# The input projection by Strassen's seven products, in two passes over paired column blocks

## What is computed

```python
h = rmsnorm(x, norm_mix_g)                      # (1024, 2048)
proj = h @ w_in                                 # (1024, 6160)
na_q, na_k, na_v, ml_q, ml_k, ml_v, ml_o, gates = split(proj)
na_out = rmsnorm(neighbourhood_attention(na_q, na_k, na_v))
ml_out = mlstm_mixer(conv(ml_q, ml_k), ml_v, sigmoid(ml_o), gates)
x = x + concat(na_out, ml_out) @ w_out          # (1024, 2048)
x = rmsnorm(x + expert_choice_ffn(rmsnorm(x)))  # 16 experts of 128 tokens
```

## Time and profile before

| | us |
|---|---|
| median of three runs | 2886.12 |
| span of the profiled execution, first to last instruction | 2884.0 |
| PE busy | 2791.8, 97% of the span |
| DVE busy | 1616.2, 56% |
| ACT busy | 1328.0, 46% |
| bytes moved | 665.67 MB, mean 231 GB/s |

### The profile page before, as it was taken

How to read it: one execution, slowest core, us unless ns; L and a number is a source line. 1 busy time by engine, 2 the same in 40 slices (tenths; PEclk the granted TensorE clock), 3 DMA queues, 4 the chain that set the end, 5 groups by cost and what they waited for, 6 DMA issues and landing times.

```text
span 2884.0 us, 33947 instructions
## 1 busy us (share of the span) xinstructions
PE 2791.8 (97%) x12906; PEld 2301.7 (80%) x12906; DVE 1616.2 (56%) x1801; ACT 1328.0 (46%) x1465; POOL 392.4 (14%) x613
## 2 busy tenths in 40 slices
PE   9999999999999999989999967999999999999997
PEld 7888888788888888767888856888888888888884
DVE  4111111321332326676345658888888888888886
ACT  6111112211111106654333334777777777777775
POOL 1200000020110024572010101000000000000002
PEclk9999999999999999999999988999999999999998
DMA  8322112121423237533444457999999999999997
GB/s 322 90 80 80 59 65 78 54 96 56 150 96 104 92 107 229 193 123 129 153 164 142 166 166 312 381 403 403 393 396 404 403 405 402 405 401 405 401 390 336
DMA packets 193313, 665.67 MB, mean 231 GB/s; under 512 B 23305, under 2 KB 48408, under 8 KB 170016
## 3 DMA queue, kind: packets, MB, share of 16 engines
q1 hardware_dynamic: 168336, 564.52, 51.6%
q0 software_dynamic: 24848, 99.46, 10.1%
HBM read 591.06 MB, written 75.76 MB: 231 GB/s over the span
## 4 chain that ended last, share of the span: by engine, by line
PE 91%; DVE 2%; POOL 2%; DMA 2%; issue 2%; ACT 1%; POOLq 0%; SPq 0%; DVEq 0%; ACTq 0%
PE ps L2275 24%; PE ps L1950 18%; PE ps L1929 6%; PE ps L1928 6%; PE ps L1930 6%; PE ps L2298 4%; PE ps L2297 4%; PE ps L2296 4%; PE ps L2202 4%; PE ps L2204 4%; PE ps L2203 4%; PE ps L2020 1%; PE ps L2000 1%; PE ps L2251 1%; DMA nak<-scr_feats 1%
## 5 line engine op out<-in xcount | busy, mean ns | idle before, releaser
L1843 DVE TENSOR_TENSOR elo<-eraw,ehi 128x2048 fp32r<-128x2048 f32 x384 | 874.2, 2291 | 131.2 <-ACT ehi L1263 124.4
L1263 ACT ACTIVATE ehi<-eraw 128x2048 fp32r<-128x2048 f32 x384 | 732.9, 1919 | 248.6 <-PE ps L2275 162.3
L1356 DVE TENSOR_TENSOR wlo<-raw,whi 128x1024 fp32r<-128x1024 f32 x95 | 116.4, 1225 | 684.5 <-ACT whi L999 684.4
L999 ACT ACTIVATE whi<-raw 128x1024 fp32r<-128x1024 f32 x95 | 100.6, 1059 | 718.8 <-PE ps L1950 381.7
L2275 PE MATMUL ps<-ehi,xh 128*128 128x512 f32 x960 | 373.6, 389 | 0.0
L2275 PE MATMUL ps<-elo,xh 128*128 128x512 f32 x960 | 373.5, 389 | 0.0
L1928 PE MATMUL ps<-whi,a_hi 128*128 128x512 f32 x768 | 299.0, 389 | 3.0 <-DVE a_lo L1377 3.0
L1930 PE MATMUL ps<-whi,a_lo 128*128 128x512 f32 x768 | 298.8, 389 | 0.0
L1929 PE MATMUL ps<-wlo,a_hi 128*128 128x512 f32 x768 | 298.8, 389 | 0.0
L2275 PE MATMUL ps<-ehi,xl 128*128 128x512 f32 x960 | 256.6, 389 | 0.0
L1950 PE MATMUL ps<-a_hi,whi 128*128 128x512 f32 x768 | 236.9, 389 | 2.2 <-DVE t L1399 1.6
(11 more groups left out here) (298 smaller groups left out, 3892.7 us busy)
## 6 DMA issues: line engine op xcount, KB each, us to landing
eraw<-in_w_gate SPq DMA_DIRECT2D x256, 512.0 KB, 6.1
eraw<-in_w_up SPq DMA_DIRECT2D x256, 512.0 KB, 8.2
eraw<-in_w_down SPq DMA_DIRECT2D x128, 1024.0 KB, 10.5
raw<-in_w_stream SPq DMA_DIRECT2D x95, 512.0 KB, 3.5
oraw<-in_w_stream SPq DMA_DIRECT2D x128, 256.0 KB, 2.6
scr_rows<-stage POOLq DMA_DIRECT2D x48, 256.0 KB, 2.3
scr_feats<-stage POOLq DMA_DIRECT2D x44, 256.0 KB, 2.3
t<-in_xT SPq DMA_DIRECT2D x16, 512.0 KB, 5.5
```

The source lines that it names most:

```text
L1263: act.activation(ehi[:, p % ERING, :], flat2(eraw[:, 2 * (p % EDEEP):2 * (p % EDEEP) + 2, :]), ACT.Copy)\
L1843: dve.tensor_tensor(elo[:, p % ERING, :], flat2(eraw[:, 2 * (p % EDEEP):2 * (p % EDEEP) + 2, :]), ehi[:, p % ERING, :].bitcast(F32), ALU.s ...
```

## The change

The twelve blocks are taken as six pairs q (1024 columns each). With the tokens, the contraction and a pair's columns each in two halves, the product of a pair is a 2x2 by 2x2 block product, and it is made by Strassen's seven products (m1 to m7) in place of eight. A product is 8 slices x 4 banks x 3 = 96 matmuls in four chunks; products use the banks 0 to 3 and 4 to 7 in turn, and a bank must be drained two products later (`bank_free`).

- Pass one makes, for q = 0 to 5, m4 = A22(B21-B11), m3 = A11(B12-B22), m2 = (A21+A22)B11, m5 = (A11+A12)B22. From these C21 = m2+m4 and C12 = m3+m5 are finished and stored, and m2-m3 and m5-m4 are parked in DRAM (`part`).
- Pass two makes, for q in the order 3, 0, 2, 4, 5, 1, m1 = (A11+A22)(B11+B22), m6 = (A21-A11)(B11+B12), m7 = (A12-A22)(B21+B22), loads the parked tiles and finishes C22 and C11.
- The combined inputs of pass two (24 pairs of slices, `ops`) are made by DVE and ACT during pass one (q = 1 to 4, six each), stored to DRAM, and loaded by POOL's queue at the chunks 88 to 103. Those of pass one are made from the loaded slices at the start, where the slices come as 128x512 tiles and the ones that are summed come two by two.
- The combined weights are made when they are needed: of 168 chunks, 120 are a sum or difference of two raw chunks (`PAIRED`), which DVE forms (`combine`, 128x1024). So 288 chunks are loaded in place of 96. `raw` stays a ring of four loads; `whi` and `wlo` are rings of three.
- The gate products stand before q = 5 of pass one; the gate arithmetic is at DVE's chunks 102 to 110 of pass two (before: in block 6), the convolution at the chunks 117, 123, ..., 159. A chunk is 24 matmuls now (before: 48).
- The loops of the projection are written out. Semaphores of early stages are used again by late ones (`LATER`, `BEFORE`). Attention's queries and keys come from q = 4 and 5; the queries are put in their order by the access pattern of PE's moving operand (`unit_order`, runs of 16 elements) and of the drain.

```diff
 BW = 512
 BLK = 12
-ROWBLK = 6
+NQ = BLK // 2
+ROWQ = 3
 OBLK = 4
+KH = KD // 2
 CPB = KD // 2
-RING = 4
-GWC = KD * 16 + 32
+RING, SPL = 4, 3
+GWC = 4 * P + 28
 QR, QC, WR, WC = 8, 16, 12, 32
...
+ORDER2 = (3, 0, 2, 4, 5, 1)
+QUERYQ = 4
+PRODS = [(a, q) for q in range(NQ) for a in ("m4", "m3", "m2", "m5")] + [(a, q) for q in ORDER2 for a in ("m1", "m6", "m7")]
+NP1, NPR = 4 * NQ, 7 * NQ
+NCH = 4 * NPR
+HALVES = {"m4": ((0, 4), (0, 0)), "m3": ((1, 0), (1, 4)), "m2": ((0, 0),), "m5": ((1, 4),),
+          "m1": ((0, 0), (1, 4)), "m6": ((0, 0), (1, 0)), "m7": ((0, 4), (1, 4))}
+LOADS = [(2 * PRODS[c // 4][1] + side, m + c % 4, c) for c in range(NCH) for side, m in HALVES[PRODS[c // 4][0]]]
...
+SLOT = {"m4": 3, "m3": 0, "m2": 2, "m5": 1, "m1": 3, "m6": 0, "m7": 2}
+OPSLOT = (3, 0, 2)
+OPAT = (0, 3, 5, 8, 11, 13)
+CONVAT = [117 + 6 * n for n in range(8)]
+DRAINED = (2, 3, 0, 1)
...
+        def chunk_used(eng, c):
+            p, m = c // 4, c % 4
+            if m == 3:
+                eng.wait_ge(S["bank_ready"], 4 * p + 4)
...
+        def drained(c):
+            p, i = (c - 2) // 4 - 1, (c - 2) % 4
+            if p < 0:
+                return None, None, None, None
+            a, q = PRODS[p]
...
+            def fetch(n):
+                b, m, c = LOADS[n]
+                if n >= RING:
+                    sp.wait_ge(S["w_lo"], LOADS[n - RING][2] + 1)
+                sp.dma_start(raw[:, n % RING, :], t["w_stream"][CPB * b + m, :, :]).then_inc(rawsem[n % RING], 16)
...
+            def fetch_slice(s):
+                hi, lo = slice_f32(s)
...
+                if s >= 2 * KH:
+                    sp.dma_start(hi, t["xT"][k * P:(k + 1) * P, half_ * BW:(half_ + 1) * BW]).then_inc(xtsem[s % 8], 16)
+                if s // KH != 1:
+                    k += KH
+                sp.dma_start(lo, t["xT"][k * P:(k + 1) * P, half_ * BW:(half_ + 1) * BW]).then_inc(xtsem[s % 8], 16)
...
+            def fetch_op(o):
+                if o >= 2:
+                    sp.wait_ge(opstsem[o % 2], 32 * (o // 2))
+                for a, (k, half_) in zip(op_tiles(o), op_slice(o)):
+                    sp.dma_start(a, t["xT"][k * P:(k + 1) * P, half_ * BW:(half_ + 1) * BW]).then_inc(opldsem[o % 2], 16)
...
+            def load_p11(r, i):
+                j = DRAINED[i]
+                sp.wait_ge(stsem[j], 16 * NQ + 16 * r)
+                sp.wait_ge(heldsem[j], 16 * (ORDER2[r] + 1))
+                sp.dma_start(stage[:, j, :], t["part"][0, ORDER2[r], j, :, :]).then_inc(xtsem[4 + j], 16)
...
+            def store_sum(q, j, i):
+                pool.wait_ge(S["sig_out" if q == ROWQ - 1 else "c21_out"], i + 1 if q == ROWQ - 1 else 4 * q + i + 1)
+                pool.dma_start(place_of(q, 0, 1, j), ring[0]).then_inc(S["c21_st"], 16)
+                pool.wait_ge(S["p22_out"], 4 * q + i + 1)
+                pool.dma_start(t["part"][1, q, j, :, :], ring[1]).then_inc(S["p22_st"], 16)
...
+            def load_operand(o, i):
+                part, k = i % 2, 2 * (i // 2)
+                if i == 0:
+                    pool.wait_ge(S["bank_ready"], 4 * (4 * (NQ - 1) + o + 1))
+                    for m in opstsem:
+                        pool.wait_ge(m, 32 * 4 * (o + 1))
+                pool.dma_start(slots[OPSLOT[o]][part][:, k:k + 2, :], t["ops"][o, part, k:k + 2, :, :].rearrange("k p c -> p k c"))\
+                    .then_inc(opinsem[o], 16)
...
+            def high(c):
+                n = FIRST[c]
+                if PAIRED[c]:
+                    act.wait_ge(S["w_sum"], SUMS[c])
+                else:
+                    act.wait_ge(rawsem[n % RING], 16 * (n // RING + 1))
+                if c >= SPL:
+                    chunk_used(act, c - SPL)
+                act.activation(whi[:, c % SPL, :], raw[:, n % RING, :], ACT.Copy).then_inc(S["w_hi"], 1)
...
+            def opened(tile, done, count):
+                act.wait_ge(S[done], count)
+                act.activation(tile, tile, ACT.Sigmoid).then_inc(S["sig_out"], 1)
...
+                if c == 102:
+                    act.wait_ge(S["gate_arg"], 1)
+                    act.activation(t2[0:64, 0:1024], t2[0:64, 0:1024], ACT.Exp, scale=-1.0).then_inc(S["act_step"], 1)
+                    step.settle()
+                    act.activation(t2[0:64, 0:1024], t2[0:64, 0:1024], ACT.Ln, bias=1.0).then_inc(S["gate_act"], 1)
...
+            def combine(c):
+                if not PAIRED[c]:
+                    return
+                for n in (FIRST[c], FIRST[c] + 1):
+                    dve.wait_ge(rawsem[n % RING], 16 * (n // RING + 1))
+                a, b = raw[:, FIRST[c] % RING, :], raw[:, (FIRST[c] + 1) % RING, :]
+                dve.tensor_tensor(a, a, b, sign(c)).then_inc(S["w_sum"], 1)
...
+            def sum_feats(q, j, i):
+                dve.wait_ge(S["bank_ready"], 4 * p1_at("m2", q) + j + 1)
+                dve.wait_ge(S["p22_st"], 16 * (4 * q + i))
+                dve.tensor_tensor(by_unit(ring[1], q), by_unit(bank_of(p1_at("m2", q), j), q), bc_for(q, 1), ALU.mult)\
+                    .then_inc(S["dve_step"], 1)
+                step.settle()
+                dve.wait_ge(S["s4_out"], 4 * q + 4)
+                dve.wait_ge(S["c21_st"], 16 * (4 * q + i))
+                dve.wait_ge(S["p11_out"], 4 * q)
+                dve.tensor_tensor(ring[0], ring[1], held[:, j, :], ALU.add).then_inc(S["c21_out"], 1)
+                dve.wait_ge(S["s3_out"], 4 * q + 4)
+                dve.tensor_tensor(ring[1], ring[1], stage[:, j, :], ALU.subtract).then_inc(S["p22_out"], 1)
...
+            def op_sum(o):
+                dve.wait_ge(S["rstd_bc_in"], 16)
+                dve.wait_ge(opldsem[o % 2], 32 * (o // 2 + 1))
+                for a, (k, half_) in zip(op_tiles(o), op_slice(o)):
+                    dve.scalar_tensor_tensor(out=a, in0=a, scalar=gmix[:, k:k + 1], in1=bc_half(half_), op0=ALU.mult, op1=ALU.mult)\
+                        .then_inc(S["dve_step"], 1)
+                step.settle()
+                step.settle()
+                a, b = op_tiles(o)
+                dve.tensor_tensor(a, a, b, ALU.add if o < KH else ALU.subtract).then_inc(S["op_sum"], 1)
...
+            def both_less(r, j, i):
+                p = p2_at("m1", r)
+                dve.wait_ge(S["bank_ready"], 4 * p + j + 1)
+                dve.wait_ge(xtsem[j], XT0 + 16 * (r + 1))
+                dve.tensor_tensor(held[:, j, :], bank_of(p, j), held[:, j, :], ALU.subtract).then_inc(S["q22_out"], 1)
+                dve.wait_ge(xtsem[4 + j], XT0 + 16 * (r + 1))
+                dve.tensor_tensor(stage[:, j, :], bank_of(p, j), stage[:, j, :], ALU.subtract).then_inc(S["q11_out"], 1)
...
+            def forget_sums():
+                dve.wait_ge(S["gate_act"], 1)
+                dve.scalar_tensor_tensor(out=T1, in0=T1, scalar=0.0, in1=T2, op0=ALU.min, op1=ALU.subtract).then_inc(S["dve_step"], 1)
...
+                dve.wait_ge(S["mask_done"], 1)
+                for r, way in ways:
+                    dve.tensor_tensor_scan(out=t1[r, ::way], data0=t3[r, :], data1=t1[r, ::way], initial=0.0,
+                                           op0=ALU.mult, op1=ALU.add).then_inc(S["dve_step"], 1)
+                    step.settle()
+            def running_maxima():
+                dve.tensor_tensor(T0, T0, T1, ALU.subtract).then_inc(S["dve_step"], 1)
...
+                dve.tensor_scalar(T3, T3, -1.0, -NEG, ALU.add, ALU.mult).then_inc(S["dve_step"], 1)
...
+            for c in range(1, NCH):
+                low(c)
+                if c + 1 < NCH:
+                    combine(c + 1)
...
+                drain(c)
+                if op_at(c, 0) is not None:
+                    op_sum(op_at(c, 0))
+                if op_at(c, 1) is not None:
...
+                if c == 102:
+                    gate_rows()
+                if c == 103:
+                    forget_sums()
+                if c == 104:
+                    running_maxima()
+                if c == 106:
+                    chunk_ends()
+                if c == 107:
+                    stabilizers()
+                if c == 108:
+                    dve.wait_ge(S["gate_act"], 3)
...
+            def bank_free(p, j):
+                i = DRAINED.index(j)
+                if p == 4 * (NQ - 1) and j < 2:
+                    pe.wait_ge(S["gates_copied"], 1)
+                if p < 2:
+                    return
+                a, q = PRODS[p - 2]
+                if p - 2 >= NP1:
+                    q = (p - 2 - NP1) // 3
+                pe.wait_ge(S[{"m4": "s4_out", "m3": "s3_out", "m2": "p22_out", "m5": "p11_out", "m1": "q11_out", "m6": "c22_out", "m7": "c11_out"}[a]],
+                           4 * q + i + 1)
...
+            def product(p):
+                a, q = PRODS[p]
+                slot = SLOT[a]
+                if p >= NP1:
+                    pe.wait_ge(opinsem[("m1", "m6", "m7").index(a)], 16 * 8)
...
+                    hi, lo = whi[:, c % SPL, at:at + BW], wlo[:, c % SPL, at:at + BW]
```

(16 more changed lines are left out.)

1166 lines of the change are left out of this document (657 added, 509 removed).

## The result

| | before | after | forecast |
|---|---|---|---|
| median, us | 2886.11 | 2905.88 (2903.43 to 2906.96) | 2794 (2766 to 2838) |
| span of the profiled execution | 2884.0 | 2901.7 | 2791.6 |
| first matmul of the projection | 8.65 | 10.24 | 7.9 |
| TensorE's end of the projection | 1079.7 | 1097.0 | 986.6 |
| time of TensorE beyond its matmuls | 3.7 | 150.1 | 42 |

After against before is 1.0064, 95% interval 1.0052 to 1.0076: slower by 0.6%, clear of the noise, where I had forecast 3.2% faster. (The median before is now that of four executions.) The matmuls are the 4032 + 96 forecast, and behind the projection nothing moved (2901.7 - 1097.0 = 1804.7, before 1804.3). But for a first matmul 2.3 us later than forecast, all of the miss lies in the 150.1 us, which are 1097.0 - 10.24 - 914.5 - 22.2. Products are numbered from 0, chunks from 0, four to a product.

What follows compares the result with a forecast made beforehand. It took the projection to be bound by its number of matmuls: 576 fewer save 130.6 us, some 42 return as stalls, so the projection ends at 986.6 against 1079.7, giving 2794 us (range 2766 to 2838).

Steps and rivals of the forecast that it cites:

- Weights in the steady state: Paired chunks' loads through the ring of four: pair landing 5.5 us, loop inside 10.9 with 1.5 to spare, costed at nothing.
- A lead of 8 us: Weight splitting on DVE: low(c) done 2.5 us into chunk c-2, a lead of 8 us taken to cover delays.
- the ring of loads becomes the bound: Rival for paired chunks: landing of 8.5 us eats the gain, 9.5 gives 2946 us; chance 0.04, 0.05 for half of it.
- even gaps before every chunk: Sign in the projection that the forecast was wrong and the ring of loads was the bound; no size given.
- Gate arithmetic: DVE's chunks from 102: PE stands 13 us at product 26, 2.4 at 27, clock loses 2.5; 18 us, bounds 5 to 35.
- Drains of pass one: Drains in products with operand work (q = 3, 4): 0 to 1 us of stall each, 3 us in all, bounds 0 to 12.
- the start: Products 0 to 3, chunks 0 to 15: loads at about 350 GB/s and slice processing cost 16 us, bounds 5 to 35.
- the convolution: Some 6 us on DVE every sixth chunk, low 3.7 us late against a lead of 8: costs nothing.
- the end: End of the projection: attention's first transposes wait for four banks between the scores, 0.7 us more than before.
- no price of runs: Moving operand at q = 4 in runs of 16: claimed free, since scores' runs of 32 cost 0.85 ns a column.
- matmuls of q = 4 longer than 0.2268: Sign in the projection's q = 4 products that the forecast was wrong; 0.2268 us is the forecast time of each matmul.
- my rival's price: Rival for q = 4's 672 matmuls: runs of 16 at half rate, 152 us more, 2946 us; chance 0.01.

## Why the prediction was wrong, point by point

**The failed step is "Weights in the steady state", which I "cost at nothing"**, with its "1.5 us to spare a loop". I had the loop right and its terms too small: issue, landing and VectorE's part. In the mean of chunks 108 to 167 of the kernel after, from the rows of VectorE and SyncE in order of time:

| part of the loop | my sum | measured |
|---|---|---|
| slot free to issue | 0 | 1.19 |
| issue to start of the sum | 5.5 | 7.12 |
| start of the sum to end of the low part | 3.8 | 4.62 |
| all, against 10.9 for two chunks | 9.3 | 12.93 |

These 60 chunks are 30 loops of 2.05 us too much: 61 us, and the rest of pass two is 60.1 over. That these two agree proves nothing by itself, since any loop over all chunks has the mean of the chunks' own time. That the loads set it is shown by the run with one load a chunk, in which the same stretch is 3.6 over. Of the 7.12 us, some 6.5 are the landing of the pair and most of the rest is the sum waiting for its turn on VectorE. With the landing alone wrong the loop would have been an estimated 10.3 us (6.5 + 3.8) and held. Each term was known in part. For the landing (5.5) I went below the loaded 7.4 us of the earlier trace rows toward the quiet 3.5 of the earlier trace rows; two tiles in flight beside stores were the loaded case. For the issue I counted SyncE's wait for a store as 2 us once, and it came in a third of the chunks, up to 5.9 us. In VectorE's part I had a drain only beside the high part; the convolution and the wait for TensorE lie in it too.

**"A lead of 8 us" was the cover for everything else, and it was not there.** My figure was for the low part. The drain for the fourth bank has less: the pair behind which it stands is issued 2.5 us into chunk 4p+6, and PE wants the bank 2.04 us into chunk 4p+8, 10.4 us later; less issue, sum and drain some 8 us are left for the landing, with VectorE on time. It was not on time: in the mean of these chunks the low part of chunk c began 4.9 us after PE began chunk c-2 and ended at 6.1, where I had it finished at 2.5.

**The page "DMA: Bandwidth & Descriptors"** of the Trainium skill (section Measured) gives 6.15 us for 1 MB; its row is for one transfer issued from GpSimd. A pair of 512 KB tiles here, issued by SyncE beside stores, landed 6.5 us after its first issue and was in use after 7.12; the measurement decides. (By my terms the page's figure gives a loop of 10.0 us and not the 10.3 that I wrote; it would hold either way, without the other two errors.)

**The rival "the ring of loads becomes the bound" is what happened**, and I gave it 0.04 (slower than before, as it is) and 0.05 for a half of it. Its mechanism was right, its condition too narrow: I let it decide by the landing alone (8.5 us), while landing, issue and the work behind the sum add up, and needed only 3.6 us together. The prices were near: it had 92 us for 0.77 us a chunk; here 60 us went at 1.0 us a chunk in pass two alone, and more in pass one and at the gates (one tile a chunk without the sum gives 19 and 26 us back there). The sign that I had named for it, even gaps before every chunk, did not show: the gaps stand before the fourth bank.

**Gate arithmetic: 18 us forecast, 38.7 measured, of which 13.1 to 13.5 its own.** The order of waits was right at one place: a long stall stands at the start of product 26, 8.8 us (I had 10). But product 26 is only 12.2 us over; product 25, for which I had nothing, is 19.0 over, and product 24 is 6.7. Without second loads and sums product 25 has no stall at all, with the sums 6.5 us. Wrong was that loads and sums would be on time beside the arithmetic. My upper bound (35, "the ring of loads late as well") names the cause, and was still too low.

**Drains of pass one: 3 forecast, 32.4 measured.** 9.7 went when the bias transfers stood later (the pair of product 9 behind them), which I hadn't looked at when they moved beside a fuller queue; with one tile and no sum 13.1 remain, 4.9 of them the operand in runs of 16. The 9.6 between are the second loads and sums elsewhere in pass one. The other 8.2 of the 13.1 stand mostly in products 4 and 12, before the tenth matmul; their cause stays open.

**Right or near:** matmuls; the start (16 forecast, 18.8 measured) and its rate, 339 GB/s, between the two of the earlier trace rows; the convolution at nothing (3.6 us over in the rest of pass two with one tile, what three products with the operand in runs take); the end (+0.7, measured +0.4). The first matmul was to be 0.8 us earlier and came 1.6 later. With one tile and no sum the projection is 46.9 us over where my sum had 42. That is in part luck: pass one has 13.1 there for my 3, the gates 13.1 for my 18, and the sums, which my forecast had in it at no cost, are left out; with them it is some 65. So the second loads are 87 of the 112 us that the time is above the forecast, and VectorE's sums 16.5.

**The operand in runs of 16**: I had "no price of runs" from the scores, which move runs of 32. It has one, 0.0127 us a matmul, 8.6 us in all at most. My sign of being wrong, matmuls of q = 4 longer than 0.2268, came true; my rival's price for it, 152 us, did not.

## What to carry to other kernels

Where a change doubles the loads per unit of work and keeps the ring, add up the whole loop (slot free, issue behind what else is in that queue, landing under the new load, every instruction up to the release) against the time of the units in flight, with the loaded landing, and treat a margin such as this one (1.5 of 10.9 us) as none. A drain that waits for a store is such work too, and holds up whatever is put behind it. For every instruction on which another engine waits, work out its own deadline through all that stands ahead of it in order; a lead found for one instruction is not the lead of the next. A cure that takes a buffer from another ring needs the same sum for that ring.
